# Whole weight rows for a first in-projection, features outermost

## The reference

```
h = rmsnorm(x, g_attn_norm)              # x: 256 x 1024
proj = h @ w_in                          # w_in: 1024 x 928
u, q_lat, kv_lat, k_r = split(proj, 512, 256, 128, 32)
y_pool = pool_mixer(u, ...)              # windowed means minus u, then a product per group
q  = rmsnorm(q_lat) @ w_q_b              # 256 -> 8 x 96, rope on 32 of 96
kv = rmsnorm(kv_lat) @ w_kv_b            # 128 -> 8 x 128
```

## Time and profile before

| | |
|---|---|
| median of three runs | 1446.83 us |
| profiled execution: span | 1447.1 us |
| TensorE busy | 1402.3 us, 97% |
| VectorE, ScalarE, GpSimd busy | 410.3, 233.3, 14.0 us |
| DMA over the span | 343 GB/s |

### The profile page before, as it was taken

One profiled execution on the slowest core, in us unless ns is written; L12 is line 12 of the kernel. 1 busy time (PEld: TensorE's weight loads), 2 busy tenths in 40 slices (PEclk: granted clock), 3 DMA queues, 4 the chain that ended last, 5 costly groups with the idle time before them and its releaser, 6 DMA issues.

```text
span 1447.1 us, 17780 instructions
## 1 busy us (share of the span) xinstructions
PE 1402.3 (97%) x7138; PEld 745.7 (52%) x7138; DVE 410.3 (28%) x988; ACT 233.3 (16%) x435; POOL 14.0 (1%) x9
## 2 busy tenths in 40 slices
PE   7999999999999999999999999999899999999999
PEld 6654444444444443343334433443288765888843
DVE  5567111211211211121112111211223763002784
ACT  2433111110110111011101110111123443000000
POOL 3000000000000000000000000000000000000000
PEclk9999999999999999999999999999999999999999
DMA  9968999999999999999999999999997425444400
GB/s 317 408 254 325 412 428 427 429 428 428 430 428 428 428 428 429 428 429 428 428 429 428 429 428 429 429 427 426 418 380 246 175 89 188 161 146 153 163 5 29
DMA packets 83468, 496.33 MB, mean 343 GB/s; under 512 B 6217, under 2 KB 47894, under 8 KB 56322
## 3 DMA queue, kind: packets, MB, share of 16 engines
q1 hardware_dynamic: 82820, 494.69, 84.1%
q10 hardware_dynamic: 606, 1.06, 0.2%
HBM read 494.68 MB, written 1.05 MB: 343 GB/s over the span
## 4 chain that ended last, share of the span: by engine, by line
PE 73%; DMA 24%; DVE 2%; issue 0%; ACT 0%; SPq 0%; DVEq 0%; ACTq 0%
PE PS L964 18%; DMA ring<-in_w_gate_up_dram 15%; PE PS L990 11%; PE PS L1356 11%; PE PS L949 6%; PE PS L1099 6%; DMA qk<-in_w_gate_up_dram 5%; PE PS L1366 5%; PE PS L998 3%; DMA ring<-in_w_ada_dram 2%; PE PS L687 2%; PE PS L1223 2%; PE PS L789 2%; PE PS L671 1%; PE PS L976 1%; PE PS L958 1%
## 5 line engine op out<-in xcount | busy, mean ns | idle before, releaser
L964 PE MATMUL PS<-ring,store 128*64 128x512 f32 x1360 | 300.9, 594 | 14.1 <-DMA ring<-in_w_gate_up_dram 13.7
L964 PEld LDWEIGHTS PS<-ring,store 128*64 128x64 f32 x1360 | 93.6, 137 | 208.8 <-issue 171.5
L2115 DVE TENSOR_SCALAR store<-PS 128x512 f32<-128x512 f32 x32 | 22.1, 691 | 623.1 <-PE PS L964 623.1
L990 PE MATMUL PS<-ring,store 128*64 128x512 f32 x704 | 154.8, 592 | 0.0
L1356 PE MATMUL PS<-xc,ring 128*128 128x256 f32 x704 | 152.3, 379 | 0.1
L1356 PEld LDWEIGHTS PS<-xc,ring 128*128 128x128 f32 x704 | 133.6, 190 | 18.9 <-issue 0.8
L949 PE MATMUL PS<-store,rows 128*128 128x64 f32 x1024 | 121.3, 272 | 0.2 <-DVE store L2093 0.2
L949 PEld LDWEIGHTS PS<-store,rows 128*128 128x128 f32 x1024 | 119.7, 192 | 1.1 <-issue 1.1
L990 PEld LDWEIGHTS PS<-ring,store 128*64 128x64 f32 x704 | 49.2, 137 | 90.8 <-issue 89.2
L1099 PE MATMUL PS<-ring,xc 128*128 128x240 f32 (+1 forms) x448 | 93.9, 366 | 0.1
L1545 ACT ACTIVATE store<-store 128x512 f32<-128x512 f32 x32 | 20.1, 629 | 452.2 <-DVE store L2115 452.2
(11 more groups left out here) (372 smaller groups left out, 1218.4 us busy)
## 6 DMA issues: line engine op xcount, KB each, us to landing
ring<-in_w_gate_up_dram SPq DMA_DIRECT2D x85, 2048.0 KB, 35.0
ring<-in_w_down_dram SPq DMA_DIRECT2D x44, 2048.0 KB, 37.2
qk<-in_w_gate_up_dram SPq DMA_DIRECT2D x20, 2048.0 KB, 37.5
ring<-in_w_ada_dram SPq DMA_DIRECT2D x24, 1024.0 KB, 13.9
store<-in_w_gate_up_dram SPq DMA_DIRECT2D x11, 2048.0 KB, 34.9
ring<-in_w_gate_up_dram SPq DMA_DIRECT2D x22, 1024.0 KB, 5.1
xc<-in_w_down_dram SPq DMA_DIRECT2D x10, 2048.0 KB, 36.4
store<-in_w_down_dram SPq DMA_DIRECT2D x10, 2048.0 KB, 37.8
```

Of the source, the lines that this page charges most:

```text
L964: mm = pe.matmul(bank(b)[CAP * h:CAP * (h + 1), :], xg[:, k, :], w[:, b * FE + h * 512:b * FE + (h + 1) * 512], start=False, stop=(k == KD ...
L990: mm = pe.matmul(bank(3)[CAP * h:CAP * (h + 1), :], lhs, w[:, (f % 2) * D + h * 512:(f % 2) * D + (h + 1) * 512], start=False, stop=(f == 7))
```

## The change

The four chunks become whole rows: chunk c holds rows of feature tiles c and c + 4, all 928 columns. A run is 3712 bytes. `project_lat` takes the chunks in order and in each both feature tiles and both row tiles, for the 416 latent columns (banks 4 and 5). Then `project_pool(0)` and `project_pool(1)` take the 512 pool columns of one row tile each (banks 7 and 6), over all four chunks. The slots go back in the last pass. ScalarE keeps four pieces (`proj_kept` counts to 4): both latent tiles, then after the sines both pool tiles. TensorE waits for the third before the modulation chunks, whose bank 7 is that of the first pool tile. The loads of the gate-up bias are issued behind chunk 3 and those of the down bias behind chunk 5. VectorE's split of the down bias comes behind the k rows. The signals `vec2_turned` and `vec2_cols` are counted on `vec_turned` and `vec_cols`.

```diff
-IN1_CHUNKS = sorted(split(IN1, CW), key=lambda c: (c[0] < D_POOL, c[0]))
+IN1_SLOTS = KD // 2
+IN1_KEPT = 4
+LAT_W = IN1 - D_POOL
...
-                a, w = IN1_CHUNKS[n - N_IN1]
-                return ins["w_in"][0][:, a:a + w].rearrange("(k p) n -> p k n", p=P), KD, w
+                return ins["w_in"][0].rearrange("(h c p) n -> c p h n", h=2, p=P)[n - N_IN1], 2, IN1
...
-                if n == 0:
+                if n == 3:
                     for i in range(3):
                         load_small(bgu_f[32 * i:32 * i + 32, :], ins["b_gate_up"][0], "bgu_in")
-                if n == 3:
+                if n == 5:
                     for i in range(3):
                         load_small(bdown_f[32 * i:32 * i + 32, :], ins["b_down"][0], "bdown_in")
...
+            def project_lat():
+                for c in range(IN1_SLOTS):
+                    need(N_IN1 + c)
+                    for h in range(2):
+                        k = c + IN1_SLOTS * h
+                        need_col(k)
+                        for t in range(NT):
+                            mm = pe.matmul(bank(4 + t)[:, 0:LAT_W], cols[:, k, t * P:(t + 1) * P],
+                                           chunk(N_IN1 + c)[:, h, D_POOL:IN1], start=(k == 0), stop=(k == KD - 1))
+                mm.then_inc(sig["in1_done"], 1)
+            def project_pool(t):
+                for c in range(IN1_SLOTS):
+                    for h in range(2):
+                        k = c + IN1_SLOTS * h
+                        mm = pe.matmul(bank(7 - t), cols[:, k, t * P:(t + 1) * P], chunk(N_IN1 + c)[:, h, 0:D_POOL],
+                                       start=(k == 0), stop=(k == KD - 1))
+                    if t == NT - 1:
+                        mm.then_inc(chunk_used, 1)
+                if t == 0:
+                    mm.then_inc(sig["in1_done"], 1)
...
-            project(IN1_CHUNKS, N_IN1, (4, 5), 0)
+            project_lat()
+            project_pool(0)
+            pe.wait_ge(sig["vec_cols"], 1)
+            project_pool(1)
...
             mm.then_inc(sig["lat_turned"], 1)
+            pe.wait_ge(sig["proj_kept"], 3)
             ada(0)
             ada(1)
...
+            act.wait_ge(sig["in1_done"], 1)
+            for t in range(NT):
+                keep_proj(t, D_POOL, IN1, 4 + t)
+            rotation()
+            act.wait_ge(sig["in1_done"], 2)
+            keep_proj(0, 0, D_POOL, 7)
+            act.wait_ge(chunk_used, N_IN1 + IN1_SLOTS)
+            keep_proj(1, 0, D_POOL, 6)
```

More of the change, by code:

```diff
@@ L102 @@
 N_IN1 = 0
-N_QB = N_IN1 + len(IN1_CHUNKS) + 2
+N_QB = N_IN1 + IN1_SLOTS + 2
 N_KVB = N_QB + 1
@@ L200 @@
 SIGNALS = """x0_in x1_in third0_in third1_in third2_in x_spread const2_in band_in vec_in vec2_in wpool_in gfin_in bada_in bgu_in bdown_in router_in
-bdown_split vec_turned vec_cols vec2_turned vec2_cols c_ready rows_ready rows_act rows_turned cols_dve cols_act proj_kept
+bdown_split vec_turned vec_cols c_ready rows_ready rows_act rows_turned cols_dve cols_act in1_done proj_kept
 lat_rows lat_turned lat_cols qkv_kept trig_arg trig_ready q_roped k_roped qk_turned q_cols k_cols
@@ L702, in _ @@
             mm.then_inc(sig["lat_turned"], 1)
+            pe.wait_ge(sig["proj_kept"], 3)
             ada(0)
             ada(1)
-            pe.wait_ge(sig["proj_kept"], len(IN1_CHUNKS))
+            pe.wait_ge(sig["proj_kept"], IN1_KEPT)
             pe.wait_ge(sig["lat_cols"], 1)
@@ L762, in _ @@
                                   gffn.rearrange("j (p k) -> j p k", k=2)[:, :, k], ident[0:4, 0:4])
-            mm.then_inc(sig["vec2_turned"], 1)
+            mm.then_inc(sig["vec_turned"], 1)
             for i in range(2, 6):
@@ L830, in _ @@
             scores(heads_1[1])
-            pe.wait_ge(sig["vec2_cols"], 1)
+            pe.wait_ge(sig["vec_cols"], 2)
             pe.wait_ge(sig["ada_kept"], 1)
@@ L1093, in in2 @@
                     if c >= 2:
-                        pe.wait_ge(sig["proj_kept"], len(IN1_CHUNKS) + c - 1)
+                        pe.wait_ge(sig["proj_kept"], IN1_KEPT + c - 1)
                     need(n)
@@ L1143, in turn_conv @@
             def turn_conv():
-                pe.wait_ge(sig["proj_kept"], len(IN1_CHUNKS) + R_CONV)
+                pe.wait_ge(sig["proj_kept"], IN1_KEPT + R_CONV)
                 pe.wait_ge(sig["heads_cols"], 3)
@@ L1290, in _ @@
             ml_values(9)
-            pe.wait_ge(sig["proj_kept"], len(IN1_CHUNKS) + N_CH)
+            pe.wait_ge(sig["proj_kept"], IN1_KEPT + N_CH)
             out2(0, 0)
@@ L1419, in _, with keep_proj @@
             act.wait_ge(sig["rows_ready"], 1)
[L1421 to L1429, removed]
+            def keep_proj(t, lo, hi, b):
+                do.tell(nc.scalar.activation(proj1[:, t, lo:hi], bank(b)[:, 0:hi - lo], ACT.Copy,
+                                             scale=stat(rs, S_ATTN)[:, t:t + 1]), "proj_kept")
             def rotation():
@@ L1435, in rotation @@
                 do.tell(nc.scalar.activation(trig[:, :, :, :], trig[:, :, :, :], ACT.Sin), "trig_ready")
-            keep_proj(proj1, IN1_CHUNKS, (4, 5), N_IN1, between={2: (rotation,)})
+            act.wait_ge(sig["in1_done"], 1)
[6 more added lines that the diff above has]
+            keep_proj(1, 0, D_POOL, 6)
             flat_q = q_rows.rearrange("p t h n -> p t (h n)")
@@ L1858, in _ @@
                                             r_[:, 2 * i + t:2 * i + t + 1], None, ALU.mult), "lat_rows")
[L1859 to L1867, removed]
             dve.wait_ge(sig["lat_turned"], 1)
@@ L1894, in _ @@
                                       proj1[:, t, IN1 - ROPE:IN1].unsqueeze(1).to_broadcast([P, HEADS, ROPE])))
+            dve.wait_ge(sig["bdown_in"], 48)
+            for hi in (96, 64, 32):
+                cast = v.tensor_copy(bdown_b[0:hi, :], bdown_f[0:hi, :])
+                if hi > 32:
+                    do.step(cast)
+                    rest = bdown_f[0:hi - 32, :]
+                    do.step(v.tensor_tensor(rest, rest, bdown_b[0:hi - 32, :], ALU.subtract))
+                else:
+                    do.tell(cast, "bdown_split")
             dve.wait_ge(sig["qkv_kept"], 3)
@@ L1911, in _ @@
                                       bank((0, 1, 4, 5)[b])[0:QK, :].rearrange("p (h t) -> p h t", h=2)), "k_cols")
-            dve.wait_ge(sig["vec2_turned"], 1)
+            dve.wait_ge(sig["vec_turned"], 2)
             do.step(v.tensor_copy(vcol[:, NVEC_FIRST:NVEC], bank(6)[:, NVEC_FIRST:NVEC]))
             do.tell(v.tensor_copy(vcol[:, GFFN_AT:GFFN_AT + KD].rearrange("p (j k) -> p j k", k=2),
-                                  bank(6)[:, GFFN_AT:GFFN_AT + KD].rearrange("p (k j) -> p j k", k=2)), "vec2_cols")
+                                  bank(6)[:, GFFN_AT:GFFN_AT + KD].rearrange("p (k j) -> p j k", k=2)), "vec_cols")
             def keep_ada(segment):
@@ L2254, in _ @@
             head_norms(0)
-            dve.wait_ge(sig["proj_kept"], len(IN1_CHUNKS) + R_GATES)
+            dve.wait_ge(sig["proj_kept"], IN1_KEPT + R_GATES)
             def bias_of(a, n):
```

## The result

| | median | lowest, highest | runs |
|---|---|---|---|
| before | 1449.09 us | 1446.13, 1452.60 | 17 |
| after | 1453.51 us | 1451.69, 1454.93 | 17 |

The ratio is 1.0029 (1.0023 to 1.0036), some 4.2 us slower. The profile of after has a span of 1451.4 us, 4.3 more than that of before. Its execution took 1453.28, 1.9 above its span, and in nearly all other executions that have both figures on record it was 1.8 to 1.9. So the 1447.1 us span of before points to an execution of about 1448.9, like the median of 17 and not like the 1446.83 of the three runs shown first. That is inferred; the execution's own time is not on record.

The account below looks back on a forecast made before the run. TensorE's chain was taken to bound the first 50 us, shifts reaching the end one to one through the expert weight stream. 1.2 us gained, 3.1 lost to clock: +1.9 on 1446.83 gives 1448.7 us; range 1442.0 to 1451.6.

Parts of the forecast that it names:

- Base: The time the predicted difference was added to: 1446.83 us, the median of the runs shown.
- Start and product: In-projection on TensorE: starts near 9.4 us, 3.8 earlier; latent pass 11.2 us, pool passes 13.7, no work saved.
- Arrivals: Weight chunks land at 9.3, 11.7, 15.9 and 18.3 us, constants at 13.5; pool passes end at 35.2.
- Bias: Gate-up bias load behind chunk 3 takes 3.1 us; GpSimd's split starts at 21.4 us instead of 16.1, onto the latents' normalisation.
- The walk: Step-by-step timing of GpSimd's casts and subtractions against VectorE's squares, from 21.4 us to latents ready at 40.5.
- Who is blocked: Latents' normalisation on VectorE: all operations, two-input ones too, held by GpSimd; latents at 40.5 us, q product 1.2 us earlier.
- The second rival: GpSimd holds only single-input VectorE operations: latents end at 37.4 us, q product gains 4.2, total 1442.6; chance 0.14.
- the third: Rival: GpSimd's bias work never delays the latents; TensorE goes on at 35.2 us, total 1440.3; chance 0.10.
- Clock: TensorE after its 5.4 us idle stretch before the latents' turns: half clock, costing 3.1 us.
- Sum: 1.2 us gained at the q product, 3.1 lost to the clock: +1.9 us, carried one to one to the end.
- Moved at no cost: Down-bias split moved behind the k rotation, before the q rotation, with 1 us of cover left; other moves free too.
- Late constants: Rival: positions land after about 18.2 us, so VectorE's constants work meets GpSimd; total 1450.9 or 1452.5; chance 0.09.

Follow-up runs that it names:

- e8: The kernel after, unchanged, run once more for a second profile: 1452.69 us, q product at 47.84 us.
- e1: The kernel after, with GpSimd's gate-up bias split waiting for the four scalings of the latents: 1447.11 us, ratio 0.9986 to before.
- e2: The kernel before, with only the bias loads moved, gate-up behind chunk 3 and down behind chunk 5: 1457.04 us, ratio 1.0046 to before.
- e4: The kernel after, with ten useless matmuls between the last pool matmul and TensorE's wait for the latents: 1451.52 us, ratio 1.0019 to before.
- e10: e6 without GpSimd's wait for the latents; later constants and cut down-bias split stay: 1451.94 us, ratio 1.0021 to before.
- e6: e1 plus constants and positions loaded behind chunk 3 and the down-bias split cut in two: 1444.45 us, ratio 0.9961 to before.
- e9: e6 plus useless early matmuls that keep TensorE busy from 3 us: 1442.72 us, ratio 0.9961 to before.
- e5: The kernel before, with six useless matmuls (2.6 us) between the modulation chunks and the q product: 1449.91 us, ratio 1.0001 to before.

## Why the prediction was wrong

The mechanism held: GpSimd held the latents' normalisation, TensorE idled, and half clock followed. The direction was called (+1.9 us) and the size was not (+4.2), and 1453.51 lies 1.9 us above the range. Two steps failed, the base that the sum was put on and the landing of the bias.

*Base.* The sum went onto the median of three runs, 1446.83. Over 17 runs the kernel before has 1449.09. This step alone is 2.3 of the 4.8 us by which the forecast of 1448.7 fell short: from 1449.09 it would have been 1451.0, and the range would have ended at 1453.9, above the measured time.

*Start and product:* right. First matmul at 9.68 (9.4 forecast), 13.90 us for the pool passes (13.7), clock 1.00 from 9.3 to 37.2.

*Arrivals:* chunks 2 and 3 were waited for until 16.98 and 20.40, not 15.9 and 18.3; the pool passes ended at 37.19, not 35.2. DMA did not hold the 407 GB/s of long loads there: 310 over 13.1 to 23.4. The 4.4 us that the projection gained were 6.4 in the sum.

*Bias:* this is the term that was mis-sized. GpSimd could start at 24.4 (24.9 in e8), not 21.4: 2.1 us from chunk 3's delay and 1 from the bias's own transfer, while DMA gave 258 GB/s from 18 to 24. All of GpSimd's work moved with it, but the latents came at 42.2, only 1.7 us later than the forecast 40.5. The walk had an error the other way: it let GpSimd wait for each square and so gave its work 15.3 us, against the 14.1 that the prediction itself had read; in the trace GpSimd's next instruction starts within 0.1 us and the five take 14.2 (24.40 to 38.59).

*Who is blocked:* right, and newly shown. Two-input operations are held like the others, four of four (0.43, 0.42, 0.29 and 0.29 us in e1). The Trainium skill, page "SBUF — State Buffer", section "Who interferes with whom", says that an operation with two SBUF inputs contends with a GpSimd instruction that reads SBUF; this trace now agrees, with 4.16 us for a 0.42 us operation. The second rival falls with it. So does the third, that all is hidden: with the bias behind chunk 3 the normalisation was held in each profile (after, e2, e4, e8, e10) but those with the added wait (e1, e6, e9).

*Clock:* right in kind; 2.0 us lost, not 3.1 (4.60 us of work for 2.60), and in e4's profile bought back; 2.4 in e8. Here errors offset: latents 1.7 us later, clock 1.1 cheaper, so that q, forecast at 46.2 with the clock in it, came at 46.88 (47.84 in e8).

*Sum:* +2.6 us at q in one profile and +3.6 in the other against +1.9, one to one up to the gather, and 1.7 or 0.2 behind it. Both sums, 4.3 and 3.8, are near the measured 4.2. The carry to the end was not quite one to one, then: the prediction had no term for the two levels behind the gather. How many of the 17 executions had which q and which level is not on record. Nor does one profile fix the kernel before: it scatters by 6.5 us, and in e5's profile its q product would have started near 42.6 without the added work. The prediction also read the chain there as TensorE's alone, where VectorE's latent columns ended 0.1 us ahead of the q product.

*Moved at no cost:* right for the down-bias split in the kernel after, whose q rotation waited 2.28 us for ScalarE and not for the split. In e1, where TensorE came earlier and GpSimd held the k rotation, the 1 us of cover that the prediction counted was not enough, and TensorE waited 1.5 us.

*Late constants:* did not happen; the casts began at 14.7 and ran free.

## What to carry to other kernels

When a load is moved, follow the engine that waits for it: here GpSimd's work on the moved bytes slid onto VectorE's critical five microseconds, and one wait turned 0.2% of loss (e10) into 0.4% of gain (e6) with the loads in the same order. Look for engines that hold each other before blaming the queues, and ask of every idle stretch on TensorE what the clock does to the work behind it. Before inserting work to test a path, look for a second engine that ends just ahead of the same instruction. And put a predicted difference on many runs of the kernel before, not on the first three.

## What the runs showed of the hardware

- GpSimd's casts and subtractions on SBUF held VectorE operations with two SBUF inputs until they ended, and in after VectorE got one instruction through for each of GpSimd's five: 1.59, 4.16, 1.85 and 4.09 us for squares that take 0.43, 0.42, 0.29 and 0.29 alone. A square that began 0.01 us ahead of a subtraction (e10) took 0.43, and the subtraction 4.34 instead of at most 4.14. Operations with a PSUM source were not: in e1 L1875, beside a cast and the start of a subtraction, took 1.52 us for three.
- While the loads of 32 rows of 8 KB ran, the core moved 220 to 258 GB/s (18 to 24 us in e1 and after, with the end of chunk 3 in it); in the stretch of whole weight rows of 3712 bytes 417 (14 to 18 us in after).
- An idle stretch of 5 us on TensorE cost 2 us of clock behind it (after), and the profile with useless matmuls in it did not have that cost (e4).
- The same idle stretch of 1.6 us near 1185 us was followed by half pace in e2, e6 and e9 and by full pace in the other nine profiles. One half pace near 10 us has a granted clock of 1.00 in the record (e6): look at the time of an instruction as well.
